# Experts of a two-block network: nineteen lasting weight slots, the gather between the down columns, a divided scatter, and the last pair by halves

## What is computed

```python
def hier_moe(h, w_rg, b_rg, w_re, b_re, w_g, w_u, w_d):
    ...
    combine = jnp.einsum('nk,nke->ne', weights,
                         jax.nn.one_hot(expert_id, N_EXPERTS, dtype=jnp.float32)).astype(h.dtype)
    y = jnp.zeros_like(hf)
    for e in range(N_EXPERTS):
        act = jax.nn.silu(hf @ w_g[e]) * (hf @ w_u[e])
        y = y + combine[:, e:e + 1] * (act @ w_d[e])
    return y.reshape(B, S, D)
```

```python
        x = x + gate2 * y_moe
```

## Time and profile before

| what | us |
|---|---|
| time, median of 3 runs (1378.8 to 1379.68) | 1379.45 |
| time of the profiled execution | 1379.51 |
| its span, first to last instruction | 1377.7 |
| expert columns on PE, first to last (L962) | 233.2 to 676.5 |
| PE busy over the span | 1329.3 |

### The profile page before, as it was taken

The page is one execution under the profiler, slowest core; times in us unless marked ns, Lnnn a source line. Parts: engine busy times, 40 slices in busy tenths (PEclk is TensorE's granted clock), DMA queues, the critical chain, the costliest instruction groups (busy, mean ns, idle before and its releaser), DMA issues.

```text
span 1377.7 us, 21079 instructions
## 1 busy us (share of the span) xinstructions
PE 1329.3 (96%) x8758; PEld 1003.9 (73%) x8758; DVE 634.7 (46%) x1423; ACT 298.0 (22%) x595; POOL 9.0 (1%) x20
## 2 busy tenths in 40 slices
PE   8999999999999988888999999999999999999997
PEld 5888886453343334333588789999998878999996
DVE  2477465121001000010378847775455784777454
ACT  2234102112111111111243521220013352122000
POOL 0000000000000000000000000000000000000000
PEclk9999999999999999999999999999999999999999
DMA  9997787899999999999954144445444414454510
GB/s 392 363 414 269 302 355 258 330 421 420 421 421 421 421 421 421 421 421 421 420 224 154 62 153 153 172 165 173 164 155 153 153 62 153 154 183 156 182 62 32
DMA packets 52545, 365.15 MB, mean 265 GB/s; under 512 B 6225, under 2 KB 6529, under 8 KB 9441
## 3 DMA queue, kind: packets, MB, share of 16 engines
q1 hardware_dynamic: 49680, 355.49, 65.5%
q10 hardware_dynamic: 1888, 5.04, 1.3%
q0 software_dynamic: 880, 3.24, 0.6%
HBM read 359.28 MB, written 2.37 MB: 263 GB/s over the span
## 4 chain that ended last, share of the span: by engine, by line
PE 83%; DMA 14%; DVE 1%; ACT 1%; issue 0%; DVEq 0%; SPq 0%
PE bank L1224 26%; PE bank L647 20%; PE bank L962 15%; DMA ring<-in_weights 10%; PE bank L659 5%; DMA ringx<-in_weights 4%; PE bank L975 2%; PE bank L1369 2%; PE bank L1160 2%; PE bank L775 2%; PE bank L947 1%; PE bank L1273 1%; PE bank L1324 1%; PE bank L719 1%; PE bank L1350 1%; PE bank L1337 1%
## 5 line engine op out<-in xcount | busy, mean ns | idle before, releaser
L962 PE MATMUL bank<-ring,cst 128*64 128x512 f32 x632 | 174.6, 594 | 13.9 <-DMA ring<-in_weights 9.8
L647 PE MATMUL bank<-h,ring 128*128 128x256 f32 x832 | 184.1, 381 | 0.1
L647 PEld LDWEIGHTS bank<-h,ring 128*128 128x128 f32 x832 | 157.2, 190 | 22.4 <-issue 1.7
L962 PEld LDWEIGHTS bank<-ring,cst 128*64 128x64 f32 x632 | 55.8, 137 | 104.1 <-issue 104.1
L1224 PE MATMUL bank<-hid,ring 128*128 128x128 f32 x912 | 115.6, 276 | 0.0
L1224 PE MATMUL bank<-h,ring 128*128 128x128 f32 x896 | 113.8, 276 | 0.0
L2144 DVE TENSOR_TENSOR act<-act,bank 128x512 f32<-128x512 f32 x16 | 11.0, 688 | 220.8 <-PE bank L962 220.8
L1224 PEld LDWEIGHTS bank<-hid,ring 128*128 128x128 f32 x912 | 108.6, 192 | 0.0
L962 PE MATMUL bank<-ringx,cst 128*64 128x512 f32 x272 | 100.6, 594 | 7.0 <-DMA ring<-in_weights 5.7
L1224 PEld LDWEIGHTS bank<-h,ring 128*128 128x128 f32 x896 | 107.0, 192 | 0.1
L962 PE MATMUL bank<-ring,a_s 128*64 128x512 f32 x328 | 92.4, 596 | 3.2 <-ACT a_s L1529 3.2
(11 more groups left out here) (397 smaller groups left out, 1846.6 us busy)
## 6 DMA issues: line engine op xcount, KB each, us to landing
ring<-in_weights SPq DMA_DIRECT2D x264, 1024.0 KB, 12.1
ringx<-in_weights SPq DMA_DIRECT2D x49, 1024.0 KB, 26.0
pool_a<-in_weights SPq DMA_DIRECT2D x9, 1024.0 KB, 26.1
x<-in_weights SPq DMA_DIRECT2D x9, 1024.0 KB, 26.0
x<-in_x SPq DMA_DIRECT2D x1, 1024.0 KB, 5.1
pool_a<-in_cst ACTq DMA_DIRECT2D x1, 1024.0 KB, 6.3
bias<-bias_rows POOLq DMA_DIRECT2D x1, 1024.0 KB, 17.0
x_all<-in_weights SPq DMA_DIRECT2D x1, 1024.0 KB, 6.7
```

Source lines behind the costliest of these rows:

```text
L647: ins = e.matmul(u.ap[:, 0:S], w[:, k * width + j * P:k * width + (j + 1) * P], acts[:, k, :], start=k == 0, stop=k == kc - 1)
L962: ins = e.matmul(g.bank[bank][ex * SLOTS:(ex + 1) * SLOTS, :], stat(m, ex), block, start=first and m == 0, stop=last and m == blocks - 1)
```

## The change

- The slots BESIDE and SPREAD go, with their patched buffers, and with them the saving and reloading of the rotary table in GpSimd's program. 20 tiles are loaded early instead of 22. AHEAD alone is used once, and now for tile 19. The same 19 slots last.
- Tiles 20 to 37 are loaded by halves (512 columns x 2 each), in groups of four DMAs a pair of tiles; after these whole tiles follow.
- KEPT now takes tile 18 and every nineteenth after it, of which the last is n = 190.
- PE: the gather moves from before the down columns to between their two tile pairs. The scatter is divided: its first half comes between gate and up, its second behind up.
- Last pair: second up tiles and second down tiles are loaded by halves with a semaphore for the second halves; the product of silu(gate) and up, the transposes and the copies go by halves; the scatter's first products stand between the last down blocks.

```diff
-AHEAD, BESIDE, SPREAD, KEPT = range(R + RX, R + RX + 4)
-FIRST_SLOTS = (R + 5, R + 3, R + 2, 0, 1, 2, 3, 4, 5, AHEAD, R, R + 1, 6, 7, 8, 9, 10, R + 4, 11, BESIDE, SPREAD, KEPT)
-ONCE = {3: SPREAD, 6: AHEAD, 7: BESIDE}
+AHEAD, KEPT = R + RX, R + RX + 1
+FIRST_SLOTS = (R + 5, R + 3, R + 2, 0, 1, 2, 3, 4, 5, AHEAD, R, R + 1, 6, 7, 8, 9, 10, R + 4, 11, KEPT)
+ONCE = {19: AHEAD}
 EARLY = len(FIRST_SLOTS)
+BY_HALVES = range(EARLY, 38)
+LAST_HALVES = {PAIRS * 12 - 6: "last_up", PAIRS * 12 - 2: "last_down"}
...
-    for h in range(2):
-        for ex in range(2):
-            t = T_EXP + EARLY + ex
-            if h:
-                slot_free(sp, g, t)
-            else:
-                sp.wait_ge(g.s["half_used"], 2)
-            sp.dma_start(g.ring[SLOT[t]][:, h * D:(h + 1) * D], w[t][:, h * D:(h + 1) * D]).then_inc(g.slot_filled[SLOT[t]], 16)
-    for t in range(T_EXP + EARLY + 2, T_LAYERS):
-        slot_free(sp, g, t)
         sp.dma_start(g.ring[SLOT[t]][:, :], w[t]).then_inc(g.slot_filled[SLOT[t]], 16)
+    for n in BY_HALVES[::2]:
+        for h in range(2):
+            for ex in range(2):
+                t = T_EXP + n + ex
+                if h:
+                    slot_free(sp, g, t)
+                else:
+                    sp.wait_ge(g.s["half_used"], 2 * ((BEFORE[t] - T_EXP) // 2 + 1))
+                part = slice(h * D, (h + 1) * D)
+                sp.dma_start(g.ring[SLOT[t]][:, part], w[t][:, part]).then_inc(g.slot_filled[SLOT[t]], 16)
+    for n in range(BY_HALVES[-1] + 1, PAIRS * 12, 2):
+        halved = LAST_HALVES.get(n)
+        first = slice(0, D if halved else TILE)
+        for t in (T_EXP + n, T_EXP + n + 1):
+            slot_free(sp, g, t)
+            sp.dma_start(g.ring[SLOT[t]][:, first], w[t][:, first]).then_inc(g.slot_filled[SLOT[t]], 16)
+        if halved:
+            for t in (T_EXP + n, T_EXP + n + 1):
+                sp.dma_start(g.ring[SLOT[t]][:, D:], w[t][:, D:]).then_inc(g.s[halved], 16)
     n = max(t for t in range(T_EXP, T_LAYERS) if SLOT[t] == KEPT) - T_EXP
     sp.wait_ge(g.s["col_b" if n % 2 else "col_a"], n // 2 + 1)
     sp.dma_start(g.x_t[:, :], g.dram["x_kept"]).then_inc(g.s["x_kept"], 16)
...
+        if p:
+            pe_scatter(e, g, p - 1, 0)
         for half in range(2):
             pe_columns(e, g, tile + 4 + 2 * half, b + 1, 4, x(half), half == 0, half == 1)
         if p:
-            pe_scatter(e, g, p - 1, 0)
-            if not last:
-                pe_scatter(e, g, p - 1, 1)
+            pe_scatter(e, g, p - 1, 1)
+        if p == PAIRS - 1:
+            break
...
+        e.wait_ge(s["a_copied"], p + 1)
+        pe_columns(e, g, tile + 8, b, EC, a, True, True)
         if p < CHUNKS - 1:
             e.wait_ge(s["pick_ready"], p + 2)
             pe_gather(e, g, 2 - b)
-        e.wait_ge(s["a_copied"], p + 1)
-        pe_columns(e, g, tile + 8, b, EC, a, True, True)
         e.wait_ge(s["put_ready"], p + 1)
         pe_columns(e, g, tile + 10, b + 1, EC, a, True, True)
...
+    for half in range(2):
+        e.wait_ge(s["a_copied"], PAIRS + half)
+        pe_columns(e, g, tile + 8, b, EC, a, True, True, (2 * half, 2 * half + 1))
+    pe_columns(e, g, tile + 10, b + 1, EC, a, True, True, (0, 1))
+    e.wait_ge(s["put_ready"], PAIRS)
+    pe_scatter(e, g, PAIRS - 1, 0, (0, 1))
+    pe_columns(e, g, tile + 10, b + 1, EC, a, True, True, (2, 3))
+    pe_scatter(e, g, PAIRS - 1, 0, (2, 3))
+    pe_scatter(e, g, PAIRS - 1, 1)
```

More of the change, by code:

```diff
@@ L228, in __init__ @@
         self.s = {n: sem(n) for n in SEMS}
-        self.slot_filled = [sem(f"slot_filled_{i}") for i in range(R + RX + 4) if i != BESIDE]
-        self.slot_filled.insert(BESIDE, self.slot_filled[AHEAD])
+        self.slot_filled = [sem(f"slot_filled_{i}") for i in range(R + RX + 2)]
         self.bank_full = [sem(f"bank_full_{i}") for i in range(8)]
@@ L309, in filled @@
     def filled(self, e, t):
-        both = [o + T_EXP for o in ONCE if ONCE[o] in (AHEAD, BESIDE)]
-        e.wait_ge(self.slot_filled[SLOT[t]], 16 * (sum(map(pieces, both)) if t in both else USE[t] + pieces(t)))
+        e.wait_ge(self.slot_filled[SLOT[t]], 16 * (USE[t] + pieces(t)))
         return self.ring[SLOT[t]]
@@ L950, in pe_gather, with pe_columns @@
             ins.then_inc(g.s["gathered"], 1)
-def pe_columns(e, g, tile, bank, blocks, stat, first, last):
+def pe_columns(e, g, tile, bank, blocks, stat, first, last, at=None):
+    halved = LAST_HALVES.get(tile - T_EXP)
     pair = [g.filled(e, tile + ex) for ex in range(2)]
-    for m in range(blocks):
+    for m in at or range(blocks):
+        if halved and m == 2:
+            e.wait_ge(g.s[halved], 32)
         for ex in range(2):
-            w = pair[ex]
-            per = blocks // len(w) if isinstance(w, tuple) else 0
-            block = w[m // per][:, m % per * 512:(m % per + 1) * 512] if per else w[:, m * 512:(m + 1) * 512]
-            ins = e.matmul(g.bank[bank][ex * SLOTS:(ex + 1) * SLOTS, :], stat(m, ex), block,
-                           start=first and m == 0, stop=last and m == blocks - 1)
-            if m == 1 and tile == T_EXP:
+            ins = e.matmul(g.bank[bank][ex * SLOTS:(ex + 1) * SLOTS, :], stat(m, ex),
+                           pair[ex][:, m * 512:(m + 1) * 512], start=first and m == 0, stop=last and m == blocks - 1)
+            if m == 1:
                 ins.then_inc(g.s["half_used"], 1)
@@ L967, in pe_columns, with pe_scatter @@
                 ins.then_inc(g.s["col_b" if ex else "col_a"], 1)
-def pe_scatter(e, g, p, half):
+def pe_scatter(e, g, p, half, at=range(4)):
     gy, put = g.gy, g.put
     e.wait_ge(g.s["gy_dve" if half else "gy_act"], p + 1)
-    for oc in range(4 * half, 4 * half + 4):
+    for oc in range(4 * half + at[0], 4 * half + at[-1] + 1):
         ins = e.matmul(g.bank[4 + oc // 2][:, (oc % 2) * S:(oc % 2 + 1) * S], gy[:, oc * P:(oc + 1) * P], put[:, :],
@@ L1021, in pe_experts @@
             pe_gather(e, g, 2 - b)
-        e.wait_ge(s["a_copied"], p + 1)
-        pe_columns(e, g, tile + 8, b, EC, a, True, True)
         e.wait_ge(s["put_ready"], p + 1)
         pe_columns(e, g, tile + 10, b + 1, EC, a, True, True)
+    e.wait_ge(s["pickw_ready"], PAIRS)
+    for tt in range(ST):
+        ins = e.transpose(g.bank[3 - b][:, tt * P:(tt + 1) * P], g.pickw[:, tt * P:(tt + 1) * P], g.c("ident"))
+    ins.then_inc(s["put_turned"], 1)
     for half in range(2):
-        pe_scatter(e, g, PAIRS - 1, half)
+        e.wait_ge(s["act_ready"], PAIRS + half)
+        for f in range(2 * half, 2 * half + 2):
+            ins = e.transpose(g.bank[b + 1 if half else 2 - b][:, f * P:(f + 1) * P], g.act[:, f * P:(f + 1) * P], g.c("ident"))
+        ins.then_inc(s["act_turned"], 1)
+    for half in range(2):
[7 more added lines that the diff above has]
+    pe_scatter(e, g, PAIRS - 1, 1)
 def pe_over(e, g):
@@ L1527, in act_experts @@
         e.activation(g.act[:, :], g.bank[b][:, :], ACT.Silu).then_inc(s["silu_done"], 1)
-        e.wait_ge(s["act_turned"], p + 1)
-        e.copy(g.a_s[:, :], g.bank[b][:, :]).then_inc(s["a_copied"], 1)
-        e.wait_ge(s["put_turned"], p + 1)
-        e.copy(g.put[:, :], g.bank[b + 1][:, 0:S]).then_inc(s["put_ready"], 1)
         if p < PAIRS - 1:
+            e.wait_ge(s["act_turned"], p + 1)
+            e.copy(g.a_s[:, :], g.bank[b][:, :]).then_inc(s["a_copied"], 1)
+            e.wait_ge(s["put_turned"], p + 1)
+            e.copy(g.put[:, :], g.bank[b + 1][:, 0:S]).then_inc(s["put_ready"], 1)
             act_place(e, g, p + 1)
+        else:
+            e.wait_ge(s["put_turned"], p + 1)
+            e.copy(g.put[:, :], g.bank[3 - b][:, 0:S]).then_inc(s["put_ready"], 1)
+            for half in range(2):
+                two = slice(half * 256, half * 256 + 256)
+                e.wait_ge(s["act_turned"], p + half + 1)
+                e.copy(g.a_s[:, two], g.bank[b + 1 if half else 2 - b][:, two]).then_inc(s["a_copied"], 1)
         for n in ("col_a", "col_b"):
@@ L2143, in dve_experts @@
         e.wait_ge(s["silu_done"], p + 1)
-        e.tensor_tensor(g.act[:, :], g.act[:, :], g.bank[b + 1][:, :], ALU.mult).then_inc(s["act_ready"], 1)
+        for two in (slice(0, 512),) if p < PAIRS - 1 else (slice(0, 256), slice(256, 512)):
+            e.tensor_tensor(g.act[:, two], g.act[:, two], g.bank[b + 1][:, two], ALU.mult).then_inc(s["act_ready"], 1)
         if p < CHUNKS - 1:
```

28 lines of the change are left out of this document (4 added, 24 removed).

## The result

| what | before | after |
|---|---|---|
| time, median (lowest to highest) | 1379.57 us (1378.8 to 1380.01, 6 runs) | 1384.48 us (1383.56 to 1386.51, 6 runs) |
| time of the profiled execution | 1379.51 us | 1383.64 us |
| its span | 1377.7 us | 1381.9 us |
| norm's products start (L634, now L631) | 687.32 | 691.75 |

The changed kernel is **slower by 0.39%**: ratio 1.0039, 95% interval 1.0027 to 1.0051. I had forecast 1380.4 us and "within 0.2%" as likeliest; the median is also just above my range (1384.0).

What follows compares the result with a forecast made beforehand. The prediction took the experts' end to be set by the last of 192 weight tiles landing, with DMA engines full from 258 on. A lead of -2.0 plus 2.9 us for the late reload, on 1379.51, gave 1380.4 us; range 1377.6 to 1384.

Steps and rivals of the forecast that it cites:

- What bounds the kernel, and what is late next: Experts end with the last weight tile's landing; then x's late reload sets the second block's start, PE at 683.1, not 679.94.
- The handover: From experts to second block: norm's products 2.9 us later, bounds 1.9 to 3.9; a rival with the upper bound had 0.10.
- The small gaps are gone, 2.9 later: Second block's first product: PE starts 3.2 us later but loses its small gaps, so the norm's products come 2.9 us later.
- The lead is 2.0 us: Beginning of the experts: tile 41 lands sooner, gaining 2.0 us, from -3.2 to 2.3.
- the half tiles' pace: Loading tiles 22 to 37 by halves: 413 GB/s, 2.54 us a tile, 40.6 us for 16.
- Rival 1: Tiles 22 to 37: halves run at 366 GB/s, the lead becomes 3.2 us of loss, 1385.6 us; chance 0.17.
- the other limit that I named, the slot of tile 22: Tile 41 waits for this slot behind the moved gather: issued at 289.2, landed at 294.6 at the soonest.
- Both limits meet there: Tile 41's landing: 294.6 at the soonest by slot, 294.8 by queue, so the lead cannot exceed 2.3 us.
- My signs for it: Lead holds with no stretch under 400 GB/s between 240 and 285; it fails if the last up tile lands at 661 or later.
- 677.4 instead of 680.1, 2.7 earlier: Last pair: divided steps end the experts at 677.4 instead of 680.1, 2.7 us earlier, with the lead left out.
- The gather's new place: Pairs 0 to 2: PE waits for ScalarE's copy of the activations, 0.45 us added a pair; the divided scatter costs nothing.
- The sum: Whole kernel: -2.0 us of lead and +2.9 us at the second block's start give +0.9 us, 1380.4 us.

Runs made afterwards that it cites:

- e1_reload: Changed kernel with tiles 190 and 191 moved one slot on, so that x can be reloaded early; 1378.56 us, ratio 0.9995 to the kernel before.
- f2_late: Kernel before with one wait added, so that x is reloaded only when PE has used tile 190; 1386.16 us, ratio 1.0046.
- e2_busy: Changed kernel with five unread products of ones keeping PE busy behind the last scatter, reload still late; 1382.38 us, ratio 1.0023 to the kernel before.
- e3_whole: Changed kernel with the reload early (as e1_reload) and tiles 22 to 37 loaded whole; 1378.24 us, ratio 0.9992 to the kernel before.
- e4_gather: Changed kernel with the reload early (as e1_reload) and the gather ahead of the down columns again; 1378.68 us, ratio 0.9994 to the kernel before.
- f1_last: Kernel before with only the last pair's part of the change, reload still early; 1378.10 us, ratio 0.9991.
- f4_split_last: f1_last with the gather divided, a quarter ahead of the down columns, the rest between the down tile pairs; 1376.96 us, ratio 0.9984 to the kernel before.

## Why the prediction was right and wrong

**What bounds the kernel, and what is late next: right.** The reload of x became what sets the start of the second block. SP issued it at 675.51 behind the last down block, the DMA engines idled before it (0 GB/s in 672 to 676, as forecast), and e1_reload took 5.9 us back by moving one tile to another slot. In the frame of the prediction, which leaves the lead out, I had PE start at 683.1; it started at 682.89, with the last up tile 0.27 us later than before (661.61 against 661.34), so at 682.6. The parts fit: reload 4.8 us (I took 5.1, f2_late again shows 4.8), tile 2.5 us behind it. The handover as a whole cost 4.16 us (below), which is above the 3.9 that I had given as its bound, and the clock is why. GpSimd's loads were no factor: issued at 678.67, they held only 17% of the engines from 682 to 683 and nothing before, so my 0.6 us for them was too much.

**"The small gaps are gone, 2.9 later": this step failed.** I priced PE's 4.5 us without work at nothing but its length. The granted clock fell to 1.2 GHz at about 683.5, and the 32 instructions took 8.86 us. The same product behind the same late reload took 7.17 at full clock (e2_busy), so the fall cost 1.7 us in the profiled execution; the medians put 2.1 us on it, and in the trace of f2_late it is 2.6. The trace of before had the warning, in rows that I did not read. There PE had less to do while the experts' tokens were being picked (busy 1.8 of the 3 us from 221 to 224), and the first gather behind that (chain, then a stretch, of the kernel before) took 6.15 us, where the gather of the earlier trace rows, with the same 32 instructions at full clock, takes 3.57:

```profile
226.62 6.15 PE bank L947 x32
```

```profile
228.00:231.00 3.00, 3.00 (x16) 3.00 (x15) 2.19 (x10) 0.00 (x0) 0.00 (x0) 0.50 0.87 353
```

By the same sum with this term, the norm's products come 2.9 - 0.5 + 1.8 = 4.2 us later in the prediction's frame, and 691.75 - 0.27 - 687.32 = 4.16 is what was measured.

**"The lead is 2.0 us": this step failed too.** It is 0.45 us of loss. The term that was mis-sized is the half tiles' pace. The first four halves were down at 243.4 (I said 244.3), but tiles 22 to 37 took 43.95 us until 287.35, 2.75 us a tile and not 2.54 (42.91 us in e1_reload and 42.54 in e2_busy, with the same program there: 2.66 to 2.75). As whole tiles, in e3_whole, they took 41.15 us from the fourth half on, 2.57 us a tile. In the stretches that is 340 GB/s in 242 to 246 and 407 to 417 after it, where I had taken 413 throughout from the earlier trace rows. These rates alone would be some 41 us; the other 3 us lie between bytes moved and tiles landed (by the stretches 17.9 MB had been moved when 16.8 MB had landed). Why the landings fall behind with halves stays open. Rival 1 thus had its sign right and its place (the queue nearly empty at 242), and on the landings the rate was below the 395 GB/s at which it decides, but not the 366 that it took. Behind it stood the other limit that I named, the slot of tile 22: issued at 289.91 (I said 289.2), and 6.3 to 7.4 us to the landing rather than 5.4. "Both limits meet there" was right, and more right than I used it: e3_whole and e4_gather each lift one of them and gain nothing. My signs for it fired: the last up tile landed at 661.61 (661 or later), and there is a stretch under 400 GB/s (340 in 242 to 246).

The Trainium skill ("DMA: Bandwidth & Descriptors", Rules for kernel authors), which asks for 1 MiB or more in a DMA, came out nearer than my row: on the landings the 512 KB halves ran at 382 GB/s (16.78 MB in 43.95 us). But e3_whole shows that following it alone brings 0.3 us here.

**"677.4 instead of 680.1, 2.7 earlier": mechanism right, size off, and the wrong end point.** From the last up tile (187) to the scatter's end it was 678.37 - 661.61 = 16.8 us, and 18.8 before: 2.0 us. Two terms are missing from my sum. I let the second up tiles wait for their transfers, but PE was the later one: from the last gate tiles on (651.71) it had 3.65 + 1.93 + 7.02 us without a break, to 664.31 and not 663.4, because half of the scatter now stands ahead of the up columns. And the down columns started at 667.19, not 666.6, behind ScalarE's two copies (put L1548, a_s L1552), while the down tiles were there at 666.61. Then the end point: what counts is the end of the columns, through VectorE's copy and its 9.7 us. f1_last has 1.3 us at the norm. For the time of the changed kernel this made no difference, as the reload came later than all of it.

**The gather's new place: right in its cost a pair.** PE waited 0.46 us for ScalarE's copy in the pairs concerned (I took 0.45), and the divided scatter cost nothing that shows. What I did not ask is whether that cost could be had back: dividing the gather takes the wait away and is worth 1.1 us (f4_split_last against f1_last).

**The sum.** I had +0.9 us. To it come 2.27 us of missing lead (2.0 forecast, and the last up tile 0.27 us late) and 1.75 us for the product at half clock (8.86 against the 7.1 of my sum); less 0.5 us for the earlier reload and 0.3 us that the part behind the norm was shorter. That is +4.1 us, and 1383.64 - 1379.51 = 4.13 is measured. The median of after stands another 0.8 us above its profiled execution; the granted clock over the whole span points to a longer stretch at the lower clock, as f2_late's profile has it (0.996 in the profiled execution, 0.993 to 0.995 in the other five), but none of those was traced, so it stays open.

## To carry to other kernels

When a buffer that is saved and reloaded takes part in a rotation, work out where its *last* use falls whenever the number of slots changes: here 19 slots and 20 early tiles instead of 22 moved it from tile 173 to tile 190, and the two lines that fix it are worth 5.9 us. An idle wait of TensorE is to be priced with the slower product behind it, not by its length alone. An idle stretch of the DMA engines is worth only what the next limit leaves: ask which slot comes next, and divide the work in front of it so that it covers a copy and frees the slots at once.

## What the runs showed of the hardware

- After a wait of 4.5 us (after) PE's granted clock fell from 2.4 to 1.2 GHz for 3.4 us *while PE was working again*; around the shorter wait of 3.7 us in f2_late (680.30 to 684.00) it was low for some 6.8 us. Against the same product at full clock (7.17 us in e2_busy) they cost 1.7 and 2.6 us, so the shorter wait cost more. Five products of ones in the gap kept the clock up.
- The first gather of the experts, behind a stretch with less work for PE (in before busy 1.8 of the 3 us from 221 to 224), took 5.2 to 5.4 us in seven profiled executions and 6.2 to 6.5 in five, with the granted clock over 224 to 232 at 0.79 and at 0.57 to 0.60.
- 512 KB transfers moved at 407 to 417 GB/s with a full queue, 1 MB transfers at 418 to 424; but counted by landings the 16 tiles by halves came at 382 GB/s in after, 391 in e1_reload and 394 in e2_busy.
- A single 1 MB transfer with an idle queue takes 4.8 us from issue to landing (in after and in f2_late alike); the one right behind it lands 2.5 us later.
